# Loading the input a second time, with features on partitions, in place of the first norm's transposes

## The reference

```python
def rmsnorm(x, g):
    xf = x.astype(jnp.float32)
    y = xf * lax.rsqrt(jnp.mean(xf * xf, axis=-1, keepdims=True) + EPS)
    return (y * g.astype(jnp.float32)).astype(x.dtype)

def mixer_ab(n, pos, w_in, gq, gk, w_gate_up, b_gate, g_gla, w_out):
    proj = n @ w_in
    (qa, ka, va, iq, ik, iw, qb, kb, vb, g_low, og) = _split(proj, AB_SIZES)
    ...

# first_block, layer 0
n = rmsnorm(h, g_mix[layer])                 # h = x, (1, 256, 1024)
h = h + mixer_ab(n, pos, w_in_ab[i], ...)    # w_in_ab[i]: 1024 x 3672
h = h + squared_relu_mlp(rmsnorm(h, g_ffn[layer]), w_up[layer], w_down[layer])
```

## Time and profile before

| what | value |
|---|---|
| time, median of 3 runs | 962.05 us (961.66 to 962.15) |
| span of the profiled execution, first to last instruction | 960.6 us |
| TensorE busy / weight loads busy | 951.7 us (99%) / 843.9 us (88%) |
| VectorE / ScalarE / GpSimd busy | 610.1 / 549.7 / 135.0 us |
| moved by DMA | 168.23 MB, mean 175 GB/s |

### The profile page before, as it was taken

One profiled execution on the slowest core, in us unless ns is written; L12 is line 12 of the kernel. 1 busy time (PEld: TensorE's weight loads), 2 busy tenths in 40 slices (PEclk: granted clock), 3 DMA queues, 4 the chain that ended last, 5 costly groups with the idle time before them and its releaser, 6 DMA issues.

```text
span 960.6 us, 14466 instructions
## 1 busy us (share of the span) xinstructions
PE 951.7 (99%) x6018; PEld 843.9 (88%) x6018; DVE 610.1 (64%) x893; ACT 549.7 (57%) x786; POOL 135.0 (14%) x44
## 2 busy tenths in 40 slices
PE   9999999999999999999999999999999999999997
PEld 7888888888888888888888888899999999999886
DVE  5997847777222667747776322476558699888643
ACT  7676547666333658847766333634555687665542
POOL 0011250000664000020000765200000000000000
PEclk9999999999999999999999999999999999999999
DMA  8554245544556452545455555364444535555541
GB/s 301 213 181 169 90 137 177 207 181 175 196 198 206 155 209 88 176 148 186 178 192 176 201 193 186 133 220 175 173 146 146 194 153 182 207 184 175 187 164 45
DMA packets 25234, 168.23 MB, mean 175 GB/s; under 512 B 2816, under 2 KB 3776, under 8 KB 5456
## 3 DMA queue, kind: packets, MB, share of 16 engines
q1 hardware_dynamic: 25024, 167.23, 48.6%
q10 hardware_dynamic: 144, 0.07, 0.0%
HBM read 166.24 MB, written 1.05 MB: 174 GB/s over the span
## 4 chain that ended last, share of the span: by engine, by line
PE 96%; DVE 2%; ACT 1%; DMA 1%; issue 0%; SPq 0%; DVEq 0%
PE bank L679 23%; PE bank L680 23%; PE bank L681 23%; PE bank L761 12%; PE bank L765 6%; PE bank L707 1%; DMA raw<-w_stream 1%; PE bank L898 0%; PE bank L815 0%; PE bank L1028 0%; PE bank L1161 0%; PE bank L819 0%; PE bank L823 0%; PE bank L1054 0%; PE bank L1036 0%
## 5 line engine op out<-in xcount | busy, mean ns | idle before, releaser
L1861 DVE TENSOR_TENSOR wlo<-raw,whi 128x2048 fp32r<-128x2048 f32 (+2 forms) x151 | 308.5, 2043 | 248.9 <-ACT whi L1248 248.7
L1248 ACT ACTIVATE whi<-raw 128x2048 fp32r<-128x2048 f32 (+1 forms) x154 | 293.4, 1906 | 152.5 <-PE bank L681 150.6
L2593 POOL TENSOR_TENSOR wlo<-raw,whi 128x1024 fp32r<-128x1024 f32 (+1 forms) x38 | 134.0, 3528 | 473.8 <-ACT whi L1248 466.5
L761 PE MATMUL bank<-nhl,whi 128*128 128x512 f32 x512 | 124.2, 392 | 0.0
L761 PEld LDWEIGHTS bank<-nhl,whi 128*128 128x128 f32 x512 | 93.9, 188 | 19.1 <-issue 0.7
L679 PE MATMUL bank<-mhi,whi 128*128 128x258 f32 x384 | 108.6, 283 | 0.0
L680 PE MATMUL bank<-mlo,whi 128*128 128x258 f32 x384 | 108.3, 282 | 0.0
L681 PE MATMUL bank<-mhi,wlo 128*128 128x258 f32 x384 | 108.3, 282 | 0.0
L679 PE MATMUL bank<-nhl,whi 128*128 128x258 f32 (+3 forms) x320 | 92.5, 289 | 0.0
L680 PE MATMUL bank<-nhl,whi 128*128 128x258 f32 (+3 forms) x320 | 91.2, 285 | 0.0
L681 PE MATMUL bank<-nhl,wlo 128*128 128x258 f32 (+3 forms) x320 | 90.5, 283 | 0.0
(11 more groups left out here) (330 smaller groups left out, 1743.2 us busy)
## 6 DMA issues: line engine op xcount, KB each, us to landing
raw<-w_stream SPq DMA_DIRECT2D x154, 1024.0 KB, 4.8
h<-x_rows SPq DMA_DIRECT2D x4, 256.0 KB, 5.1
raw<-w_stream SPq DMA_DIRECT2D x2, 512.0 KB, 6.4
cst<-consts SPq DMA_DIRECT2D x1, 832.0 KB, 6.4
out_rows<-e SPq DMA_DIRECT2D x3, 256.0 KB, 2.0
e<-g_post SPq DMA_DIRECT2D x1, 512.0 KB, 3.2
raw<-w_stream SPq DMA_DIRECT2D x1, 352.0 KB, 9.6
vec<-vectors SPq DMA_DIRECT2D x1, 258.5 KB, 8.9
```

What stands on the lines that cost most here:

```text
L761: return pe.matmul(us[c].t[:, :], w[:, k, c * P:c * P + P].hi, nboth[:, k, :], start=k == 0, stop=k == 7)
L1248: act.activation(whi[j][:, 0:n], raw[j][:, 0:n], ACT.Copy).then_inc(s_hi.up(i))
L1861: dve.tensor_tensor(wlo[j][:, 0:m], raw[j][:, 0:m], whi[j][:, 0:m].bitcast(F32), ALU.subtract).then_inc(s_lod.up(i))
L2593: pool.tensor_tensor(wlo[j][:, m:n], raw[j][:, m:n], whi[j][:, m:n].bitcast(F32), ALU.subtract).then_inc(s_lop.up(i))
```

## The change

`x` is handed over a second time as `x_cols`, laid out by the host with features on partitions: 8 columns of the gain, then eight blocks k of 256 positions. It goes to the space of `QKE`, which is used only later. It comes in five parts (`FIRST_PARTS`: k = 0, 1, 2-3, 4-5, 6-7), each followed by the part of the weight tiles 0 and 1 with the same k; the first part of the weights is issued by ScalarE in place of the small piece of `vec`. The 16 transposes of the first norm, the three `keep_warm` matmuls behind the first half of them and their PSUM banks are gone; `first_hi` and `first_lo` split the blocks from SBUF. The first projection goes through k = 0 to 4 in order, with its three parts for both halves of the positions, and through k = 5 to 7 as before. The rows of `x`, which `row_stats` and the later addition to `h` need, are loaded in two transfers behind all of this, and behind them the small piece of `vec` (now without `g_mix0`), tile 2, `cst`, the gate's weights and the rest of `vec`.

```diff
@@ -26,6 +26,7 @@
 GATE_ROWS = 64
 SLOT = 2048
 NSLOT = 3
+FIRST_PARTS = [(0, 1), (1, 2), (2, 4), (4, 6), (6, 8)]
 AHEAD = 2
 BIGNEG = -1.0e30
@@ -539,7 +538,10 @@
         RSB = A(256)
         IQv = IQ.rearrange("p (t h d) -> p t h d", t=2, h=9)
         QA = xn.rearrange("p t (h d) -> p t h d", h=8)
-        QKE = A(8 * 512).rearrange("p (l n) -> p l n", l=8)
+        qke = A(8 * 512)
+        QKE = qke.rearrange("p (l n) -> p l n", l=8)
+        xc = qke[:, 0:8 + 8 * S]
+        g_first, XT = xc[:, 0:8], xc[:, 8:8 + 8 * S].rearrange("p (k t) -> p k t", k=8)
         IW = small[:, 16:32]
         ssA = small[:, 32:48].rearrange("p (j t h) -> p j t h", j=2, t=2)
...
         def n_ready(t, k):
+            if t == 0:
+                return s_xlo.at(k)
             if k % 2 == 0:
                 return s_nlo.at(t, k // 2)
             return use["tr", t, k // 2].gone() if t < 4 else s_nodd.at(k // 2)
+        def part_of(k):
+
+            return next(n for n, (a, b) in enumerate(FIRST_PARTS) if a <= k < b)
+
         def h_ready(t):
             if t == 0:
-                return [[(s_x[tt][c], 16) for c in range(2)] for tt in range(2)]
+                return [[(s_x[tt], 16)] * 2 for tt in range(2)]
             return [[use["out", t - 1, 2 * tt + c].gone() for c in range(2)] for tt in range(2)]
...
@@ -801,16 +812,14 @@
             on.wait_ge(*s_am0.at(0))
-            keep_warm(use["tr", 0, 2].t, AM[:, 0:P], AM[:, 0:256], 4)
-            half_turn(0, 0)
-            keep_warm(use["tr", 0, 2].t, AM[:, 0:P], AM[:, 0:256], 3)
+            keep_warm(use["rowf",].t, AM[:, 0:P], AM[:, 0:256], 4)
             def first_proj():
                 us = [begin("pj", 0, 0), begin("pj", 0, 1)]
                 w = [weights(i, 4) for i in range(2)]
                 def high(k, tt):
-                    on.wait_ge(*s_nhi.at(0, k))
+                    on.wait_ge(*s_xhi.at(k))
                     on.wait_ge(*s_hi01.at(k // 4, k % 4))
                     pe.matmul(us[tt].t[:, :], nTa[:, k, tt * P:tt * P + P].hi, w[k // 4][:, k % 4, :].hi, start=k == 0, stop=False)
...
@@ -822,13 +831,7 @@
                     weights_in(k // 4, k % 4)
                     return pe.matmul(us[tt].t[:, :], nTa[:, k, tt * P:tt * P + P].hi, w[k // 4][:, k % 4, :].lo, start=False, stop=k == 7)
-                for k, tt in product(range(2), range(2)):
-                    high(k, tt)
-                half_turn(0, 1)
-                for part in (low_rows, low_weights):
-                    for k, tt in product(range(2), range(2)):
-                        part(k, tt)
-                for k in range(2, 5):
+                for k in range(5):
                     for part in (high, low_rows, low_weights):
                         for tt in range(2):
                             x = part(k, tt)
...
@@ -1248,12 +1252,17 @@
                 act.activation(whi[j][:, 0:n], raw[j][:, 0:n], ACT.Copy).then_inc(s_hi.up(i))
             def hi01(i, c):
-                on.wait_ge(*((s_w, 16) if i == 0 and c >= 2 else (s_raw[i], 16)))
+                on.wait_ge(s_wc[part_of(4 * i + c)], 16)
                 act.activation(whi[i][:, c * 512:c * 512 + 512], raw[i][:, c * 512:c * 512 + 512], ACT.Copy).then_inc(s_hi01.up(i, c))
+
+            def first_hi(k):
+                on.wait_ge(s_xc[0], 16)
+                on.wait_ge(s_xc[part_of(k)], 16)
+                act.activation(nTa[:, k, :].hi, XT[:, k, :], ACT.Copy, scale=g_first[:, k:k + 1]).then_inc(s_xhi.up(k))
             def evac_turn(t, q, dst):
                 u = use["tr", t, q]
-                on.wait_ge(*(TI if t == 0 else TV))
+                on.wait_ge(*TV)
                 on.wait_ge(*u.done())
                 for kk in range(2):
                     k = 2 * q + kk
...
                     act.activation(xn[:, tt, :], h[:, tt, :], ACT.Square, accum_out=ss[:, tt:tt + 1]).then_inc(own.up())
                 on.wait_ge(*own.last())
-                on.wait_ge(*TV)
+                on.wait_ge(*TI)
                 act.activation(ss, ss, ACT.Ln, bias=eps, scale=1.0 / D).then_inc(own.up())
                 on.wait_ge(*own.last())
                 act.activation(lnrs, ss, ACT.Copy, scale=-0.5).then_inc(s_stat.up(t, 0))
...
@@ -1295,18 +1304,9 @@
             tables("natural_log_exp_and_others")
-            evac_turn(0, 0, nTa)
-            hi01(0, 0)
-            hi01(0, 1)
-            evac_turn(0, 1, nTa)
-            evac_turn(0, 2, nTa)
-            hi01(0, 2)
-            hi01(0, 3)
-            evac_turn(0, 3, nTa)
-            hi01(1, 0)
-            hi01(1, 1)
-            hi01(1, 2)
-            hi01(1, 3)
+            for k in range(8):
+                first_hi(k)
+                hi01(k // 4, k % 4)
             row_stats(0)
             rs = stats[0][2]
             on.wait_ge(*s_stat.at(0, 2))
...
@@ -1865,6 +1865,12 @@
                 on.wait_ge(*s_hi01.at(i, c))
                 dve.tensor_tensor(wlo[i][:, s], raw[i][:, s], whi[i][:, s].bitcast(F32), ALU.subtract).then_inc(s_lo01.up(i, c))
+            def first_lo(k):
+                o = nTa[:, k, :]
+                on.wait_ge(*s_xhi.at(k))
+                dve.scalar_tensor_tensor(out=o.lo, in0=XT[:, k, :], scalar=g_first[:, k:k + 1], in1=o.hi.bitcast(F32),
+                                         op0=ALU.mult, op1=ALU.subtract).then_inc(s_xlo.up(k))
+
             def evac_turn(t, q, dst):
                 u = use["tr", t, q]
                 on.wait_ge(*s_nhi.at(t, 2 * q + 1))
...
@@ -1897,18 +1903,9 @@
-            evac_turn(0, 0, nTa)
-            lo01(0, 0)
-            lo01(0, 1)
-            evac_turn(0, 1, nTa)
-            evac_turn(0, 2, nTa)
-            lo01(0, 2)
-            lo01(0, 3)
-            evac_turn(0, 3, nTa)
-            lo01(1, 0)
-            lo01(1, 1)
-            lo01(1, 2)
-            lo01(1, 3)
+            for k in range(8):
+                first_lo(k)
+                lo01(k // 4, k % 4)
             rs = stats[0][2]
             on.wait_ge(*TI)
             on.wait_ge(*s_stat.at(0, 2))
...
@@ -2594,6 +2591,12 @@
+        def first_weights(eng, n):
+            a, b = FIRST_PARTS[n]
+            i, s = a // 4, slice(a % 4 * 512, a % 4 * 512 + (b - a) * 512)
+            src = W[starts[i]:starts[i + 1]].rearrange("(p n) -> p n", p=P)
+            eng.dma_start(raw[i][:, s], src[:, s]).then_inc(s_wc[n], 16)
+
         def sync_program(sp):
             on = Once(sp)
@@ -2610,13 +2613,15 @@
                             on.wait_ge(*s_lop.at(i - NSLOT))
                 sp.dma_start(raw[j][:, 0:n], src).then_inc(s_raw[j], 16)
-            first = W[0:starts[1]].rearrange("(p n) -> p n", p=P)
-            for c in range(2):
-                for tt in range(2):
-                    sp.dma_start(h[:, tt, c * 512:c * 512 + 512], X[tt * P:tt * P + P, c * 512:c * 512 + 512]).then_inc(s_x[tt][c], 16)
-                sp.dma_start(raw[0][:, c * 1024:c * 1024 + 1024], first[:, c * 1024:c * 1024 + 1024]).then_inc(s_w if c else s_raw[0], 16)
-            for i in range(1, NSLOT):
-                stage(i)
+            for n, (a, b) in enumerate(FIRST_PARTS):
+                s = slice(8 + a * S if a else 0, 8 + b * S)
+                sp.dma_start(xc[:, s], XC[:, s]).then_inc(s_xc[n], 16)
+                if n:
+                    first_weights(sp, n)
+            for tt in range(2):
+                sp.dma_start(h[:, tt, :], X[tt * P:tt * P + P, :]).then_inc(s_x[tt], 16)
+            sp.dma_start(vec[:, o_id:NVEC], V[:, o_id:NVEC]).then_inc(s_i, 16)
+            stage(2)
             sp.dma_start(cst[:, 0:o_masks], C[:, 0:o_masks]).then_inc(s_c, 16)
             sp.dma_start(wg, WG).then_inc(s_c, 16)
             sp.dma_start(vec[:, 0:o_id], V[:, 0:o_id]).then_inc(s_v, 16)
...
@@ -2651,7 +2656,7 @@
         @block.scalar
         def _(eng):
-            eng.dma_start(vec[:, o_id:NVEC], V[:, o_id:NVEC]).then_inc(s_i, 16)
+            first_weights(eng, 0)
             scalar_program(eng)
         @block.vector
...
@@ -2763,6 +2768,7 @@
     a = {k: np.asarray(v) for k, v in inputs.items()}
     c, dlx, cm, tri = constants()
+    x_cols = a["x"][0].T.reshape(8, P, S).transpose(1, 0, 2).reshape(P, 8 * S)
     arrays = {
         "w_stream": weight_stream(a),
         "vectors": vectors(a),
...
@@ -2771,6 +2777,7 @@
         "consts_m": cm,
         "tri": tri,
         "x_rows": np.ascontiguousarray(a["x"][0]),
+        "x_cols": np.concatenate([a["g_mix"][0].reshape(8, P).T, x_cols], axis=1),
         "meta_rows": np.ascontiguousarray(a["meta_tokens_2"]),
         "gate_up": np.concatenate([a["w_gate_up"][0], np.zeros((GATE_ROWS - 16, 256), np.float32)]),
         "g_post": np.ascontiguousarray(np.broadcast_to(a["g_ffn_post_2"][0][None, :], (P, D))),
```

More of the change, by code:

```diff
@@ L35 @@
     ("conv_b_mix", 4), ("g_mix_post", 8), ("g_ffn_pre", 8), ("conv_w_ffn", 132), ("conv_b_ffn", 44),
-    ("gq_row", 128), ("gk_row", 128), ("g_mix0", 8), ("eps", 1),
+    ("gq_row", 128), ("gk_row", 128), ("eps", 1),
     ("ident", 128),
@@ L314, in feat @@
```

(19 more changed lines are left out.)

## The result

| | time, us | runs |
|---|---|---|
| before | 962.06 (961.66 to 962.29) | 7 |
| changed | 964.62 (963.98 to 965.73) | 7 |

The account below looks back on a forecast made before the run. The prediction took TensorE, busy 99%, as the bound, so only a shift of its wait-free stretch counts. Tile 3 begun 0.7 us later, added to the median of 962.05, gave 962.7 us, range 961.1 to 964.3.

Parts of the forecast that it names:

- Where the change can act: TensorE's whole stream: the change touches the first 20 us alone and can shift the stream but not shorten it.
- First projection, begin near 6, end near 17: TensorE's first projection, fed by x_cols and weights in parts, was to end 3.2 us earlier than before.
- Rows of x at 14.7, row_stats to 17.65, tile 2 at 19.45: Row-factor chain ahead of tile 2: it releases tile 2's products, 0.86 us earlier than 20.31.
- one of the prediction's own signs of being wrong: Landing of x's rows: the prediction counts as wrong if they land well before 14 or after 16 us.
- Tile 3, the term that decided: 1028 KB added ahead of tile 3: landing at 19.6 instead of 17.93, TensorE starting it 0.7 us later.
- The sum's 360 GB/s for the small transfers: Within tile 3's landing: rate for tile 2 with the small transfers, 0.871 MB, so 2.42 us.
- From a last byte to the landing I take 1.0 us: Lag from last byte moved to landing, read at vec before; for tile 3, 18.6 to 19.6.
- From the landing to TensorE 4.34: Tile 3's copy, difference and two hand-offs: landed at 19.6, begun by TensorE at 23.94.
- Nothing is lost later: Behind tile 3: TensorE never runs dry again, so a later start moves everything behind it equally.
- The DMA debt is larger: Rival at tile 3: landing after 20.8, at 365 GB/s or less from 8 us, slower by over 1.9 us; chance 0.15.
- The 358 GB/s: Main-memory rate per core, as a lower limit from 8 us on: tile 3 lands at 21.0, loss 2.1 us.
- TensorE slows down in its pauses: Rival: half pace for 3.4 us behind the pause ahead of tile 3, 1.7 us more, 964.4; chance 0.03.

Follow-up runs that it names:

- a2: Changed kernel with four warming matmuls in TensorE's pause ahead of block 2 of the first projection; 965.79 us.
- a3: Changed kernel with tile 4's transfer issued only when tile 3 has landed; 964.51 us.
- a11: Changed kernel with x_cols in one transfer of 8 KB rows ahead of the weights, which keep their five parts; 963.06 us.
- a4: Changed kernel with tile 3 copied and differenced in four pieces, TensorE waiting for each piece; 962.34 us.
- a6: Changed kernel with the rest of vec (258.5 KB) issued behind tile 3 instead of ahead of it; 964.86 us.
- a5: Changed kernel with the first projection's inputs in two parts of four blocks instead of five parts; 964.19 us.
- a1: Kernel before the change, with x_cols (1028 KB, five transfers) also loaded between tiles 1 and 2 and not used; 963.24 us.
- a8: Changed kernel with another unused load of 1020 KB, in four transfers, ahead of tile 2; 966.99 us.
- a7: Changed kernel with tile 3 in four pieces, rest of vec behind tile 3, ScalarE taking the first projection's results ahead of tile 3's copy; 962.46 us.
- a9: Changed kernel with two first parts instead of five and 7 more warming matmuls ahead of the first projection; 962.86 us.
- a12: Changed kernel with x_cols in one transfer, 7 more warming matmuls ahead of the first projection, and tile 3 in four pieces; 961.60 us.
- a10: Changed kernel with two first parts, 11 warming matmuls, tile 3 in pieces, projection results ahead of tile 3's copy, rest of vec behind tile 3; 963.07 us.

## Why the prediction was right or wrong

- *Where the change can act: right.* The stream behind tile 3 moved as a whole: 25.52 - 23.35 = 2.17 us at tile 3, 2.2 in the spans.
- *First projection, begin near 6, end near 17: begin 0.7 early (5.29), end wrong (20.3).* Its parts were costed by the bytes up to the last one only; that the third part of `x_cols` would come at 8.20 and the weights behind it at 9.5, and stop TensorE for 2.02 us, was not seen, nor the half pace behind it. It cost nothing (a2, a3): tile 3 was later still.
- *Rows of x at 14.7, row_stats to 17.65, tile 2 at 19.45: 0.6 to 1.6 us early.* The second half came at 16.3, which was one of the prediction's own signs of being wrong (after 16); the statistics ended at 18.27, and tile 2 began at 20.39, behind the projection and not behind `lo(2)`. Again tile 3 covered it.
- *Tile 3, the term that decided: its mechanism right, its size wrong.* It had two steps. The last byte was put at 18.6; by the windows it was moved by 8 + (6.118 - 1.668)/0.397 = 19.2, since only 1.668 MB had moved by 8 us and not 1.808, and 397 GB/s followed, not the 407 that the sum comes to. (The sum's 360 GB/s for the small transfers had been read across the hole at 13 to 14 us; without that it would have come out earlier still.) Then "From a last byte to the landing I take 1.0 us": it was 2.0. That is the step that failed: the 1.0 had been read at `vec`, in the kernel before, whose engines were 1.2 us apart there, and was taken over for a queue whose engines were 2.0 apart. Both errors, 0.6 and 1.0, come from the parts of `x_cols` at the start: with `x_cols` whole (a11) the last byte comes at 18.3 by its windows (156, 337, 422, 373 and 422 GB/s for 4 us each) and the landing 0.9 later, as the prediction had taken them.
- *From the landing to TensorE 4.34 (19.6 to 23.94): right (4.32, from 21.20 to 25.52).*
- *Nothing is lost later: right for the changed kernel's profiled execution, wrong where tile 3 is used early* (a4: 1.04 us at 39.8) *and where the pace falls behind the wait* (a2, a3, a6: 1.5 us).
- *The rivals.* "The DMA debt is larger" came true in its landing (after 20.8), by a cause like one that it named, the small rows at the very start, though the engines came apart at the third part, with rows of 2 KB, and not at the two with rows of 1 KB. It didn't come true by its rate: 365 GB/s or less from 8 us on never showed, with 389 to 411 in the windows. The 358 GB/s of the Trainium skill's page "DMA: Bandwidth & Descriptors" (Specifications) gave 964.2, near the result by accident. "TensorE slows down in its pauses" had 0.03 and is real: in the changed kernel in its projection, where it cost nothing; in a5, where it cost the whole gain; and in a2, a3 and a6 at the very place that the rival names, behind the wait ahead of tile 3, where it cost 1.5 us (1.7 in the rival).

So of the 2.56 us about 1.1 are the bytes (a1; a11 has 0.85 with the slow pace in it), and the rest, about 1.5, goes to the form in which they came first. That is a difference between kernels that also differ otherwise, so an estimate. What within that form makes one engine late, row size, count or order, stays open.

## What to carry to other kernels

A transfer lands with its slowest engine: read the rate and the spread of the 16 engines, not the rate alone, and try few transfers with long rows at the head of a queue that will not run dry (a5, a11). An early start for an engine is worth nothing as long as a later tile's landing decides (a2), and bytes ahead of that tile cost their full time once the queue has no hole (a8). When a landing can't be moved, cut the first use into pieces; then look where the next chain takes the gain back (a4). And when the runs of one kernel fall in two groups, ask which group the profiled execution belongs to before setting its marks beside another's (a2, a3, a6).

## What the runs showed of the hardware

- Engines that had come 2.75 us apart (third part of `x_cols`, 5.45 to 8.20) were still 2.0 apart 13 us later. In before, where the queue had run dry at 13 to 15 us, 1.2 us at `vec` became 0.6 at tile 3. With the five parts of `x_cols` at the head (changed, a2, a3, a4, a6, a7, a8) tile 3's engines were 1.6 to 2.8 us apart in the profiled executions, with larger first transfers (a5, a9 to a12) 0.3 to 0.8. Rows of 2 KB alone don't do it: before has them in its first transfers of `x`, with 0.7 to 1.3.
- TensorE's pace halves behind some pauses: 0.43 us from start to start for 12 matmuls behind 3.41 us (a5), for 6 behind 3.33 (a11). Behind 1.74 us ahead of block 2 it didn't (a3). In the changed kernel it came 1.5 us after the end of the pause of 2.02 us. The granted clock shows it in some windows (0.50, 0.59, 0.77, 0.84) and reads 1.00 in others with the same pace.
- With 7 more warming matmuls at the start the time around the span grew, in some runs, from 1.8 to as much as 2.6 (a12), 3.2 (a10) or 3.3 us (a9). No profile shows that time, and the cause is open.
